# Short series of unread identity products in TensorE's queue, in a one-core decoder step

## The reference

```python
def run_trunk(x, c, ...):
    for layer in range(2):
        sh, sc, gt = ada_mod(c, ada_mix_w[layer], ada_mix_b[layer])      # silu(c) @ w + b, three parts
        hm = rms_norm(x, g_pre_mix[layer]) * (1 + sc) + sh
        mix = multiscale_pool(hm, ...) if layer == 0 else dilated_attention(hm, ..., w_q, w_o)
        x = x + gt * rms_norm(mix, g_post_mix[layer])
        sh, sc, gt = ada_mod(c, ada_ffn_w[layer], ada_ffn_b[layer])
        hf = rms_norm(x, g_pre_ffn[layer]) * (1 + sc) + sh
        f = swiglu(hf, ...) if layer == 0 else moe_swiglu(hf, ...)       # 2 of 8 experts
        x = x + gt * rms_norm(f, g_post_ffn[layer])
        if layer == 0: k, v = split(rms_norm(x, g_kv) @ w_kv)            # shared keys and values
```

## Time and profile before

| | |
|---|---|
| median of 3 executions | 1728.03 us (1725.89 to 1729.34) |
| profiled execution | 1726.33 us, span 1724.5 us from first to last instruction |
| mean granted clock | 0.953 |
| PE busy | 1586.0 us, 92% of the span |
| DVE busy | 1247.3 us, 72% |
| ACT busy | 981.1 us, 57% |
| chain that ended last | PE 79%, DVE 9%, DMA 4%, POOL 3%, ACT 2%, issue 2% |

### The profile page before, as it was taken

The page is one execution under the profiler, slowest core; times in us unless marked ns, Lnnn a source line. Parts: engine busy times, 40 slices in busy tenths (PEclk is TensorE's granted clock), DMA queues, the critical chain, the costliest instruction groups (busy, mean ns, idle before and its releaser), DMA issues.

```text
span 1724.5 us, 22944 instructions
## 1 busy us (share of the span) xinstructions
PE 1586.0 (92%) x8712; PEld 1303.2 (76%) x8712; DVE 1247.3 (72%) x1088; ACT 981.1 (57%) x881; POOL 141.3 (8%) x133
## 2 busy tenths in 40 slices
PE   6889999799898678699999999999999999999991
PEld 3579999598785455488888888888888888888881
DVE  4455543668783533578888888888888888889884
ACT  2244432433232432377777777877877777777771
POOL 0000000025531421100000000000000000000001
PEclk9799999899899879699999999999999999999996
DMA  9895544945568127589999999999999999999972
GB/s 344 303 337 180 180 159 152 343 143 201 166 226 312 59 68 287 206 316 374 374 390 378 355 395 382 363 388 372 381 384 366 382 387 354 395 378 370 383 275 89
DMA packets 248396, 513.05 MB, mean 298 GB/s; under 512 B 8999, under 2 KB 68567, under 8 KB 248319
## 3 DMA queue, kind: packets, MB, share of 16 engines
q1 hardware_dynamic: 241015, 490.27, 79.2%
q0 software_dynamic: 4912, 17.67, 2.7%
q10 hardware_dynamic: 2400, 4.17, 0.7%
HBM read 498.19 MB, written 14.35 MB: 297 GB/s over the span
## 4 chain that ended last, share of the span: by engine, by line
PE 79%; DVE 9%; DMA 4%; POOL 3%; ACT 2%; issue 2%; POOLq 0%; ACTq 0%; DVEq 0%
PE wide L466 23%; PE wide L467 22%; PE wide L468 22%; POOL phase L1830 2%; DVE phase L1523 2%; PE wide L517 1%; DMA ring<-in_ada_ffn_w 1%; PE wide L528 1%; PE wide L901 1%; DVE w_lo L1753 1%; POOL phase L1836 1%; PE wide L503 1%; DMA ring<-in_cache_v 1%; ACT w_hi L1236 1%; DMA ring<-in_ada_mix_w 1%
## 5 line engine op out<-in xcount | busy, mean ns | idle before, releaser
L1753 DVE TENSOR_TENSOR w_lo<-ring,w_hi 128x2048 fp32r<-128x2048 f32 x336 | 768.3, 2291 | 116.0 <-ACT w_hi L1236 114.6
L1236 ACT ACTIVATE w_hi<-ring 128x2048 fp32r<-128x2048 f32 x336 | 643.3, 1919 | 212.6 <-PE wide L468 212.5
L466 PE MATMUL wide<-w_hi,xe_hi 128*128 128x512 f32 x896 | 355.7, 397 | 5.9 <-DVE xe_lo L1758 4.1
L468 PE MATMUL wide<-w_hi,xe_lo 128*128 128x512 f32 x896 | 350.3, 391 | 0.0
L467 PE MATMUL wide<-w_lo,xe_hi 128*128 128x512 f32 x896 | 349.7, 390 | 0.0
L396 DVE TENSOR_TENSOR w_lo<-ring,w_hi 128x2048 fp32r<-128x2048 f32 (+1 forms) x58 | 139.1, 2401 | 111.1 <-ACT w_hi L965 110.8
L466 PE MATMUL wide<-tHi,w_hi 128*128 128x264 f32 x672 | 198.6, 295 | 20.4 <-DVE mLo L1441 20.4
L467 PE MATMUL wide<-mLo,w_hi 128*128 128x264 f32 x736 | 212.7, 289 | 0.0
L466 PEld LDWEIGHTS wide<-w_hi,xe_hi 128*128 128x128 f32 x896 | 168.8, 188 | 43.8 <-DVE w_lo L1753 6.2
L468 PEld LDWEIGHTS wide<-w_hi,xe_lo 128*128 128x128 f32 x896 | 168.5, 188 | 35.9
L467 PEld LDWEIGHTS wide<-w_lo,xe_hi 128*128 128x128 f32 x896 | 169.0, 189 | 33.3
(11 more groups left out here) (286 smaller groups left out, 1696.7 us busy)
## 6 DMA issues: line engine op xcount, KB each, us to landing
ring<-in_moe_w SPq DMA_DIRECT2D x336, 1024.0 KB, 6.9
ring<-in_ffn_w SPq DMA_DIRECT2D x30, 1024.0 KB, 5.4
ring<-in_ada_mix_w SPq DMA_DIRECT2D x24, 1024.0 KB, 8.6
ring<-in_ada_ffn_w SPq DMA_DIRECT2D x24, 1024.0 KB, 12.0
ring<-in_w_q SPq DMA_DIRECT2D x12, 1024.0 KB, 9.4
ring<-in_cache_k SPq DMA_DIRECT2D x24, 512.0 KB, 5.0
ring<-in_cache_v SPq DMA_DIRECT2D x24, 512.0 KB, 6.6
ring<-in_w_kv SPq DMA_DIRECT2D x8, 1024.0 KB, 6.4
```

The lines of the kernel that those rows point to most:

```text
L466: pe.matmul(out, a[0], b[0], start=start, stop=False, skip_group_check=True)
L468: return pe.matmul(out, a[1], b[0], start=False, stop=stop, skip_group_check=True)
L1236: act.activation(w_hi[:, (NSPLIT + k) % PAIRS, :], ring[:, slot, :], ACT.Copy).then_inc(hi_done, 1)
L1753: dve.tensor_tensor(w_lo[:, i, :], ring[:, slot, :], w_hi[:, i, :].bitcast(F32), ALU.subtract).then_inc(lo_done, 1)
```

## The change

A helper `keep_busy(b, n)` issues n products of `ident_r` by `ident_r` (128 moving columns) into columns 384 to 511 of bank b, with start and stop set and no semaphore. Nothing reads that range. It is called ahead of the sums 2 to 6 of the norms (16, 8, 24, 8 and 24 products), ahead of the feed-forward stage and of the query products (48 each), in the prompt loop for p from 2 to 7 between `score_step(p, 0)` and `weights_to_columns(p - 2, 1)` (8 each), ahead of the router (32), and behind the wait for the gates, ahead of the first `turn_rows` (40, in bank 2). That is 296 products. Nothing is removed and no wait is moved.

```diff
+            def keep_busy(b, n):
+
+                for _ in range(n):
+                    pe.matmul(bank[b][:, 384:512], ident_r[:, :], ident_r[:, :], start=True, stop=True)
+
             def norm_sum(i):
 
+                keep_busy(7, (0, 0, 16, 8, 24, 8, 24)[i])
                 for k in range(KC):
                     if k % (KC // 2) == 0:
                         pe.wait_ge(sq_ready, 2 * i + 2 * k // KC + 1)
...
+            keep_busy(7, 48)
             i0 = firsts[("w1", 0)]
             for c in range(FB // 2):
...
             ada_columns(2, 5)
+            keep_busy(7, 48)
...
                 if p == 1:
                     sample_turn()
+                if 2 <= p < KC:
+                    keep_busy(7, 8)
                 if 2 <= p < KC + 2:
                     weights_to_columns(p - 2, 1)
...
             ada_columns(3, 5)
+            keep_busy(7, 32)
 
 
             pe.wait_ge(h_ready, 8)
...
             pe.wait_ge(gate_taken, 1)
             pe.wait_ge(moe_ready, 1)
+            keep_busy(2, 40)
 
             def turn_rows(e, c, ahead):
```

## The result

The changed kernel takes 1747.93 us (median of 5 executions, 1745.07 to 1752.99) where the kernel before takes 1729.29: a ratio of 1.0111, 95% interval 1.0095 to 1.0128, that is +19 us. Forecast were 1739 us and at most 1747. The profiled execution is the median one, 1747.93 us with a span of 1746.1 us, and its mean granted clock is 0.945 (0.953 before). A time at 0.50 counts half, so this is about 192 us of the span at 0.50, where it was about 162: the products that fill PE's waits go with more slow time, not less.

The account below looks back on a forecast made before the run. PE's own work was taken to bound the experts, over half the span, so any delay to their start is paid in full. Terms 1.2 + 2.0 + 0 + 1.8 + 2.1 + 5.2 gave +12.3 us, 1739 us, range 1722 to 1747.

Parts of the forecast that it names:

- Price: Every added fp32r product was said to cost 112 ns at clock 1.00 and 214 ns at 0.50.
- cheap: Rival for all series: the weight load costs nothing more, 59 ns a product, 118 at half; +2 us, about 1730; chance 0.08.
- plain f32 rate: Rival for all series: products take 216 ns, 432 at half clock; +21 us, about 1749; chance 0.08.
- The clock neither held nor raised: In all series: the clock does not rise on the products, and where it falls today it falls within them; chance 0.52.
- The rival that holds and raises it: For all series: the products hold and raise the clock; -4 us, about 1724; chance 0.24.
- Norms: Series ahead of the norms' sums: norm 4 +1.2 us for overrunning 0.70 us idle; norms 2, 3 and 5 nothing.
- Norm 6: 24 products ahead of its sum: the same 1.2 us, but three waits for modulation slabs follow, so 0.
- Router and experts: 32 products ahead of the router +2.1 us; 40 ahead of the experts' turns +5.2, bounds +3.6 and +6.7; all at 0.50.
- Query products: 48 products ahead of them end before the idle time does, even with 19 at 214 ns: 0, bounds -2.2 and +0.9.
- Feed-forward: 48 products ahead of the stage, 20 done before the clock falls at 98.03: +2.0 us, bounds -1.3 and +2.9.
- Prompt loop: Series of 8 ahead of step 1's scores: 0.60 us each on the path, three iterations, +1.8 us, bounds 0.5 and 4.8.
- Turns and gates: Stretch between the router and the end of the gates, 705 to 725 us: no term, growth 0.

Follow-up runs that it names:

- the plain f32 products: Every series of the changed kernel with half as many plain f32 identity products: 1.0022; only series of 24, 24, 16 and 9 in idle time: 0.9976, against the kernel before.
- the whole: The changed kernel as it stands, all 296 products, against the kernel before: 1747.93 us, ratio 1.0111.
- the whole again: The changed kernel run a second time, unaltered, against the kernel before: ratio 1.0111 (1.0087 to 1.0135).
- the run with the loop's series moved: The changed kernel with the prompt loop's six series moved into the idle time ahead of the values' products, against the kernel before: 1.0073, +12.6 us.
- the late series: Only the prompt loop's series of 8, the router's 32 and the experts' 40 added to the kernel before: 1.0076, +13.1 us.

## Why the prediction was wrong: the steps one by one

The sign, the price of a product and the reading that these products neither hold nor raise the clock were right, and the size was not: +19 us for +12.3. A part of the distance from 1739 to 1747.93 is the base. The 12.3 us were added to the profiled 1726.33; on the kernel before as it was measured beside the changed one, 1729.29, they give 1741.6. The other 6.3 us are growth that the terms missed.

- *Price.* Right: 113 ns at 1.00 and 215 at 0.50 for the forecast's 112 and 214. The Trainium skill's 81 ns for such a chain ("TensorE: Matmul & The Clock Gate", Back-to-back issue gap) does not hold for these fp32r products; the measurement decides. The rivals "cheap" and "plain f32 rate" fall with it.
- *The clock neither held nor raised.* Right. 6.9 us of products ahead of the router and 8.6 us ahead of the experts left it at 0.50, and it rose at 722.27 in the transposes behind, as at 709.02 before. The rival that holds and raises it falls for these products. That density is the reason was argued in the prediction; the plain f32 products, which raise the clock at the same pace of starts, and the feed-forward's fp32r products, which raise it too, speak for it and do not prove it.
- *Norms.* Right within 0.2 us: norm 4 took 1.1 of the forecast 1.2, norms 2, 3 and 5 nothing. Norm 6: the 0.4 to 0.9 us of the table are 0.4 to 0.8 in runs without a norm's series as well, so its 0 stands.
- *Router and experts.* Right: +1.9 for 2.1, and +5.2 for 5.2, measured alone as 1.0030. The clock's rise behind the experts' start comes later in both executions of the whole and adds 1.0, which is inside the term's bounds.
- *Query products.* Inside their bounds, and the detail hangs on the clock. In the first execution of the whole 39 of the 48 ran at 0.50 where 19 were reckoned, no idle time was left, and the stage grew by 0.9 us; in the whole again 24 did, 0.4 us were left, and it did not grow.
- *Feed-forward.* Mis-sized: +4.2 for +2.0, outside its bounds. The step that failed is "If it falls at 98.03 as now, 20 are done". The clock fell at 94.22, 0.2 us into the series and not 2.2, 46 of the 48 took 213 ns, and the series lasted 10.07 us where 8.2 were reckoned, which is 1.8 of the missing 2.2. The other 0.4 is "with the slow start behind it as long as now": it lasts 3.8 us (104.06 to 107.87) for 2.83. The moment of the fall was read from one execution as if it were fixed. Where it fell as late as in the kernel before, in the run with the loop's series moved, 21 products ran at 1.00 and the 48 took 8.2 us, as reckoned; the growth there was 2.5 us, of which the series is 1.8 and a longer slow start 0.7.
- *Prompt loop.* Mis-sized: +4.7 alone for +1.8. The step "DVE waits for PE ... so the other 0.60 is on the path" failed, since DVE does not wait for PE behind a series of 8: DVE's scalings beside POOL's additions take 0.84 us longer in each of three iterations (2.5 us) and cover the 0.60. POOL, which waits for the very turn that the series delays, was not in the sum. In both executions of the whole the iteration of p = 2, which the forecast let go free, pays 0.7 in the same way. The rest of the 4.7 is not traced. In single executions it is a series or scores that fall at 0.50, as the ones with 3.4 and 3.6 us, but no series of the loop alone ran at 0.50 in its trace.
- *Turns and gates.* A term that was missing: +3.1 and +1.9 in the two executions of the whole. The gates' broadcast stands on the path, and the clock decides its time. PE's timeline of the changed kernel:

```profile
733.17 1.87 PE L875 MATMUL wide<-phase,const 9*8 9x512 f32 x2
734.98 2.07 PE L874 MATMUL wide<-phase,mT 9*128 9x512 f32 x2
736.98 1.87 PE L875 MATMUL wide<-phase,const 9*8 9x512 f32 x2
```

  The same groups without the loop's series:

```profile
726.34 1.02 PE L873 MATMUL wide<-phase,const 9*8 9x512 f32 x2
727.29 1.12 PE L872 MATMUL wide<-phase,mT 9*128 9x512 f32 x2
728.34 1.87 PE L873 MATMUL wide<-phase,const 9*8 9x512 f32 x2
```

  The clock fell at 732.51 in the first, ahead of most of the broadcast, and at 728.40 in the second, at its end; before it fell at 722.67, at its end too. The experts' 40 alone, with nothing changed ahead of the gates, gave +3.1 here as well, and the whole without the loop's series -0.4. So this is mostly the draw of an execution, and the profile of before was a lucky one.

With 4.2 for the feed-forward, some 4.5 for the loop (its 6.5 less the 2.1 that it grew by without its series), 1.9 to 3.1 for the gates and 1.0 for the experts' slow start in their places, the sum is 12.3 + 2.2 + 2.7 + 1.9 to 3.1 + 1.0, or 20 to 21 us, where 19 were measured. The ±2 us that the prediction allowed for the clock's steps were too few: the gates alone vary by 3 between executions. That the draws of the profiled execution of before were favourable at the gates and in the loop is chance, which the forecast could not see in one trace. What stays open is how much of the loop's 9 us inside the whole is such chance; 4.7 alone, 13.1 with the late series and 19.2 in the whole agree within their intervals.

## What to carry to other kernels

Here a filler on TensorE paid only where it moved the clock and, for the most part, ended before the engine's next work was ready; reckon its length at the lower clock too, since that is where most of the large series ran. Whatever stands ahead of a transpose in the queue delays the engine that reads the transpose, so follow that engine too, POOL among them, and ask what it will then run beside. A clock's rise or fall that a term hangs on is to be read from several executions, not from one.

## What the runs showed of the hardware

Two series with the same starts, 112 to 113 ns apart at 1.00, act differently on the clock. With fp32r identity products (an estimated 59 ns of stream in 113) it stayed at 0.50 through 32 products in 6.9 us and 40 in 8.6 us. With plain f32 ones (an estimated 108 of 113) it rose within them, after 5.1 us in the rows above. The Trainium skill ("TensorE: Matmul & The Clock Gate", Part 1, What you observe) has a run of 128-column products go from slow to fast within itself; the plain f32 products here agree, the fp32r ones of the same shape do not. And a PE that is busy in the profile's rows, as for all 13.65 us from 94.22 to 107.87, is no sign of a clock at 1.00.

DVE's scaling of 128 by 256 values in SBUF takes 0.35 us alone and 1.12 beside a POOL addition, and that of 128 by 128 takes 0.28 and 1.08. The Trainium skill ("SBUF — State Buffer", Who interferes with whom) says that DVE's `tensor_scalar` and POOL can contend for a shared pair of ports, where the one that starts second waits for the other's whole instruction; the rows agree, as both scalings end within 0.15 us of the POOL addition beside them.
